# Two gate rows by way of DRAM and the rotary half-head swap by transfers within SBUF, in a four-layer block kernel

## What is computed

```python
x = x + gt1[:, None, :] * y
h = _modulate(_rmsnorm(x, norm_g[i, 1]), sh2, sc2)
x = x + gt2[:, None, :] * (jnp.square(jax.nn.relu(h @ mlp_w1[i])) @ mlp_w2[i])
```

```python
return jnp.concatenate([x1 * c - x2 * sn, x1 * sn + x2 * c], axis=-1).astype(x.dtype)
```

## Time and profile before

| | us |
|---|---|
| median of 3 runs | 1351.86 (1350.39 to 1352.41) |
| the profiled execution, its own time | 1350.53 |
| its span in the profile | 1348.8 |
| TensorE busy | 1303.3 |
| VectorE busy | 948.8 |
| ScalarE busy | 701.5 |
| GpSimd busy | 128.3 |

### The profile page before, as it was taken

The page is one execution under the profiler, slowest core; times in us unless marked ns, Lnnn a source line. Parts: engine busy times, 40 slices in busy tenths (PEclk is TensorE's granted clock), DMA queues, the critical chain, the costliest instruction groups (busy, mean ns, idle before and its releaser), DMA issues. The chain is left out here.

```text
span 1348.8 us, 24952 instructions
## 1 busy us (share of the span) xinstructions
PE 1303.3 (97%) x10507; PEld 1129.8 (84%) x10507; DVE 948.8 (70%) x1433; ACT 701.5 (52%) x1211; POOL 128.3 (10%) x133
## 2 busy tenths in 40 slices
PE   4999999999999999999999999999999999999997
PEld 2998888998899897788888887888888998888886
DVE  1887788976768776675566888666656677756655
ACT  2544544434567555564444648654445566644443
POOL 0000000010200764100000042000000021000000
PEclk9999999999999999999999999999999999999999
DMA  9996799995341012356665532465555543565561
GB/s 362 372 363 237 299 356 380 352 343 167 115 156 64 4 35 97 95 176 201 188 189 176 182 113 91 148 206 192 187 190 160 174 139 126 172 188 194 183 197 50
DMA packets 177575, 256.90 MB, mean 190 GB/s; under 512 B 10488, under 2 KB 122552, under 8 KB 177464
## 3 DMA queue, kind: packets, MB, share of 16 engines
q1 hardware_dynamic: 177464, 255.31, 56.8%
HBM read 254.25 MB, written 1.05 MB: 189 GB/s over the span
## 5 line engine op out<-in xcount | busy, mean ns | idle before, releaser
L1514 DVE TENSOR_TENSOR w_lo<-stage,w_hi 128x1024 fp32r<-128x1024 f32 (+1 forms) x372 | 447.6, 1239 | 160.4 <-ACT w_hi L889 160.0
L889 ACT ACTIVATE w_hi<-stage 128x1024 fp32r<-128x1024 f32 (+1 forms) x378 | 380.1, 1049 | 211.7 <-PE acc L2318 191.9
L2316 PE MATMUL acc<-w_hi,z_hi 128*128 128x512 f32 x640 | 252.6, 395 | 1.6 <-DVE z_lo L1963 1.6
L2318 PE MATMUL acc<-w_hi,z_lo 128*128 128x512 f32 x640 | 249.4, 390 | 0.0
L2317 PE MATMUL acc<-w_lo,z_hi 128*128 128x512 f32 x640 | 249.2, 389 | 0.0
L2259 PE MATMUL un<-h_both,w_hi 128*128 128x256 f32 x736 | 214.3, 291 | 1.8 <-POOL w_lo L860 1.1
L2260 PE MATMUL un<-h_both,w_hi 128*128 128x256 f32 x736 | 208.1, 283 | 0.0
L2261 PE MATMUL un<-h_both,w_lo 128*128 128x256 f32 x736 | 208.0, 283 | 0.0
L2259 PEld LDWEIGHTS un<-h_both,w_hi 128*128 128x128 f32 x736 | 140.8, 191 | 9.5 <-issue 5.4
L2316 PEld LDWEIGHTS acc<-w_hi,z_hi 128*128 128x128 f32 x640 | 120.1, 188 | 27.8 <-issue 4.0
L2260 PEld LDWEIGHTS un<-h_both,w_hi 128*128 128x128 f32 x736 | 141.0, 192 | 1.2 <-issue 0.7
(11 more groups left out here) (393 smaller groups left out, 1886.0 us busy)
## 6 DMA issues: line engine op xcount, KB each, us to landing
stage<-in_mlp_w SPq DMA_DIRECT2D x64, 1024.0 KB
ada_buf<-in_ada_w SPq DMA_DIRECT2D x48, 1024.0 KB, 11.4
stage<-in_w_up SPq DMA_DIRECT2D x32, 1024.0 KB
stage<-in_w_down SPq DMA_DIRECT2D x32, 1024.0 KB
stage<-in_conv_w_in SPq DMA_DIRECT2D x12, 1024.0 KB
stage<-in_rw_w_rkv SPq DMA_DIRECT2D x12, 1024.0 KB
stage<-in_w_in_a SPq DMA_DIRECT2D x8, 1024.0 KB
stage<-in_w_kv_b SPq DMA_DIRECT2D x8, 1024.0 KB
```

The source lines that it names most:

```text
L889: A_(w_hi[u % 2][:, half, 0:n], stage[u % NSTAGE][:, half, 0:n], ACT.Copy).then_inc(hi_made, 1)
L1514: V.tensor_tensor(w_lo[u % 2][:, half, 0:n], stage[u % NSTAGE][:, half, 0:n], w_hi[u % 2][:, half, 0:n].bitcast(F32), ALU.subtract).then_i ...
L2316: MM(y, z_hi[:, kt, q], wh[:, i, :], start=(first and kt == 0), stop=False, skip_group_check=True)
L2318: ins = MM(y, z_lo[:, kt, q], wh[:, i, :], start=False, stop=(last and kt == KT - 1), skip_group_check=True)
```

## The change

The two gate rows of the first layer are no longer made by `row_of_columns`. After unit 8 of the convolution (slot 8) and after slot 26 of the first MLP, TensorE turns the eight columns into an 8 x 128 tile in PSUM, ScalarE copies that to `gate_tiles`, SyncE writes it to DRAM (ahead of units 15 and 33) and reads it back spread over 128 partitions (ahead of units 18 and 44). VectorE waits for `gate_spread` instead of `row_out`.

The eight rotation products on TensorE (two passes each) go. Instead SyncE moves the halves of heads within SBUF, four transfers of 32 partitions for each r, from `rope_in` to the new `rope_turned`. The sign moves into the sine table. The waits that the rotations brought on TensorE go with them. Three semaphores of VectorE waiting for itself become the chained wait that it uses elsewhere, and the constant table has a part of zeros (`still`) where the rotation matrix was.

```diff
+        SWAPPED_AHEAD = (U_KI + 6, U_KI + 7, U_KI + 8, U_KI + 9, U_QA + 6, U_QA + 7, U_OA + 4, U_OA + 5)
...
+        GATE_SETS = (2, 5)
+        GATE_AT = (8, 26)
+        GATE_KEPT_AT, GATE_SPREAD_AT = (15, 33), (18, 44)
...
+            def keep_gate(r):
+
+                sp.wait_ge(sem("row_out"), r + 1)
+                sp.dma_start(gate_kept[r].rearrange("(t q) -> t q", q=P), gate_tiles[:, :]).then_inc(sem("gate_written"), 16)
+
+            def spread_gate(r):
+
+                sp.wait_ge(sem("gate_written"), 16 * (r + 1))
+                sp.dma_start(gate_rows[r][:], gate_kept[r].unsqueeze(0).to_broadcast([P, D])).then_inc(sem("gate_spread"), 16)
+
+            def swap_halves(r):
+
+                n = 1 if r == ROPE_KI else 2
+                sp.wait_ge(un_free, freed(V_A + ROPE_USE[r]))
+                for g in range(4):
+                    to, src = 32 * g, 32 * (g ^ 1)
+                    sp.dma_start(rope_turned[r % 2][to:to + 32, 0:n, :], rope_in[r % 2][src:src + 32, 0:n, :]).then_inc(sem(f"rope_landed{r % 2}"), 16)
...
+                if u in GATE_KEPT_AT:
+                    keep_gate(GATE_KEPT_AT.index(u))
+                if u in GATE_SPREAD_AT:
+                    spread_gate(GATE_SPREAD_AT.index(u))
+                if u in SWAPPED_AHEAD:
+                    swap_halves(SWAPPED_AHEAD.index(u))
                 load_unit(u)
...
-            def rope(r, n, dst, bank=misc):
-                dve.wait_ge(rot_done, r + 1)
-                link(V.tensor_tensor(dst, bank[:, 0:n, :], bc4(sin_root, n), ALU.mult))
+            def rope(r, n, dst):
+                dve.wait_ge(sem(f"rope_landed{r % 2}"), 64 * (r // 2 + 1))
+                link(V.tensor_tensor(dst, rope_turned[r % 2][:, 0:n, :], bc4(sin_root, n), ALU.mult))
                 dve.wait_ge(cos_done, r + 1)
                 V.tensor_tensor(dst, dst, rope_c[:, 0:n, :], ALU.add).then_inc(rope_done, 1)
...
+            def turn_gate(r):
+
+                i = ADA_ORDER.index(GATE_SETS[r])
+                c0 = 8 * (GATE_SETS[r] % 6)
+                pe.wait_ge(ada_added, i + 1)
+                nc.tensor.transpose(ada_turns(i)[0:KT, 0:P], mods[0][:, c0:c0 + KT], ident).then_inc(row_done, 1)
...
-                if j == 9:
-                    pe.wait_ge(ada_added, 3)
-                    row_of_columns(0, mods[0][:, 16:24], acc[0], acc[1])
...
-            def rot(r, n, v):
-                pe.wait_ge(un_free, freed(v))
-                if r:
-                    pe.wait_ge(rope_done, r)
-                MM(misc[:, 0:n, :], rot_w, rope_in[r % 2][:, 0:n, :], start=True, stop=True).then_inc(rot_done, 1)
```

More of the change, by code:

```diff
@@ L45 @@
            "c", "final_g", "g_attn_a_2", "g_kv_2", "g_attn_b_2", "g_mlp_2", "g_final_2")
-CONST_PARTS = ((("ident", P), ("mean", P), ("ones", P), ("rot", P)),
+CONST_PARTS = ((("ident", P), ("mean", P), ("ones", P), ("still", P)),
                (("head_ones", P), ("head_mean", P), ("level_t", 6 * CHUNK), ("masks", 2 * CHUNK), ("eye", CHUNK), ("resets", SEQ),
@@ L92, in constant_table @@
     put("cos", np.tile(np.cos(ang), (4, 1)))
-    put("sin", np.tile(np.sin(ang), (4, 1)))
+    put("sin", np.tile(np.sin(ang), (4, 1)) * np.where(i % HD < HD // 2, -1.0, 1.0)[:, None])
     tok = np.arange(QT)[None, :, None] * P + i[:, None, None]
@@ L98, in constant_table, with build @@
     return t
-def build(nc, A, out):
+def build(nc, A, out, gate_kept):
     with ExitStack() as ctx:
@@ L162, in build @@
         c_rep = new("c_rep", [P, KT, 32])
+        gate_tiles = new("gate_tiles", [KT, P])
         def c_(name):
@@ L167, in c_ @@
             return const[i][:, lo - CONST_AT[i]:hi - CONST_AT[i]]
-        ident, mean_w, ones_w, head_ones, head_mean, rot_w = (c_(n) for n in ("ident", "mean", "ones", "head_ones", "head_mean", "rot"))
+        ident, mean_w, ones_w, head_ones, head_mean = (c_(n) for n in ("ident", "mean", "ones", "head_ones", "head_mean"))
         level_t = c_("level_t").rearrange("p (j q) -> p j q", j=6)
@@ L275, in build @@
         rope_in = [at(f"rope_in{i}", [P, 2, SEQ], r_off[3] + 2048 * i) for i in range(2)]
+        rope_turned = [at(f"rope_turned{i}", [P, 2, SEQ], tmp_off + 4096 + 2048 * i) for i in range(2)]
         rope_c = at("rope_c", [P, 2, SEQ], r_off[3] + 4096)
@@ L1043, in row_copy, with gate_out @@
                 A_(gate_rows[r][:, HALF:D], flat(high), ACT.Copy).then_inc(row_out, 1)
+            def gate_out(slot):
+                if slot in GATE_AT:
+                    r = GATE_AT.index(slot)
+                    act.wait_ge(row_done, r + 1)
+                    if r:
+                        act.wait_ge(gate_written, 16 * r)
+                    A_(gate_tiles[:, :], ada_turns(ADA_ORDER.index(GATE_SETS[r]))[0:KT, 0:P], ACT.Copy).then_inc(row_out, 1)
             def z_split(zc, j):
@@ L1070, in mlp @@
                             split_half(uu + 2, 1)
[L1071 to L1072 removed]
                         if m == 0:
                             copy_set(COPIED_AT.get(S_MLP + 2 * UPD * g + j))
+                            gate_out(S_MLP + 2 * UPD * g + j)
                         if g == 0 and m >= 2:
@@ L1609, in residual @@
                     g = gated_f if n == N_FIN1 else gated
-                    dve.wait_ge(row_out, row + 1)
+                    if row < len(GATE_SETS):
+                        dve.wait_ge(gate_spread, 16 * (row + 1))
+                    else:
+                        dve.wait_ge(row_out, row + 1)
                     link(V.tensor_tensor(g[:, k % 2, :], y, gate_rows[row][:, HALF * h:HALF * (h + 1)], ALU.mult))
@@ L2158, in rope_query @@
             def rope_query(j):
-                rope(ROPE_Q + j, 2, q_fm[:, 2 * j:2 * j + 2, :], un[(V_A + 5 + j) % 2])
+                rope(ROPE_Q + j, 2, q_fm[:, 2 * j:2 * j + 2, :])
             rope_query(0)
             select(rounds - rounds // 2)
-            V.tensor_scalar(sel_bias[:], score[:], 0.5 * TAKEN, NEG, ALU.is_gt, ALU.mult).then_inc(sem("keys_chosen"), 1)
-            dve.wait_ge(sem("keys_chosen"), 1)
+            link(V.tensor_scalar(sel_bias[:], score[:], 0.5 * TAKEN, NEG, ALU.is_gt, ALU.mult))
             pair_logits(0, 0)
@@ L2451, in turn_set @@
                     pe.wait_ge(ada_added, i)
+                for r in range(len(GATE_SETS)):
+                    if i == ADA_ORDER.index(GATE_SETS[r]) + 2:
+                        pe.wait_ge(row_out, r + 1)
                 for b in range(2):
@@ L2463, in ada_piece @@
                     turn_set(TURNED_AT[slot])
+                if slot in GATE_AT:
+                    turn_gate(GATE_AT.index(slot))
             def mlp(m, n):
```

52 lines of the change are left out of this document (13 added, 39 removed).

## The result

The changed kernel takes 1371.94 us, median of 4 runs (1371.13 to 1372.32), beside 1351.12 (1350.14 to 1352.41) for the kernel before on the same chip: a ratio of 1.0154, interval 1.0142 to 1.0166, or +20.8 us. The forecast was +14.0 and 1364.5, with a range that ended at 1372: the measured time lies at the very end of it. The sign, the place and the order of the terms hold; every term of the rope stretch was too small. The profiled execution took 1372.08, its span 1370.3.

What follows compares the result with a forecast made beforehand. The prediction took VectorE's ropes 4 to 7, made late by their swaps, to bound the stretch from 798 to 829 us. Gates -2.2, ropes +14.0 and clock +2.2 gave +14.0 on 1350.53: 1364.5 us, range 1353 to 1372.

Steps and rivals of the forecast that it cites:

- What bounds the kernel: Between 798 and 829 us VectorE's finishing of ropes 4 to 7 sets the end, not TensorE, though TensorE is 97% busy.
- Gates, -2.2: Gate rows 0 and 1 through DRAM instead of sixteen TensorE matmuls each: -2.2 us, bounds 0 and -3.6.
- The two steps: Savings on TensorE for each gate row: 0.7 us for row 0, 1.6 us for row 1, rounded together to -2.2.
- Ropes 0 to 3, 0: Removing the first four rotations from TensorE gives nothing, since VectorE is the chain at 798; bound 3.4 us.
- L: Time from issue of the load ahead of a swap to landing of its last transfer: 5.6 us, bounds 3.7 and 7.1.
- Ropes 4 to 6: Delays from late swaps, each from L and fixed distances: rope 4 +5.0 us, rope 5 +2.2, rope 6 +3.8.
- Rope 7, +3.0: Rope 7 starts later because its swap stands behind the load of U_KI+13: +3.0 us, range 1.1 to 4.5.
- The clock, +2.2: TensorE runs at half clock after the last pause ahead of ropes 4 to 7: +2.2 us, 0 to 4.4.
- the rival with 0.09: Clock falls after each of four pauses, and three other 2.2 us reach the chain: 1371 us; chance 0.09.
- Edits at nothing: Chained wait, VectorE's sine product reading SBUF instead of PSUM, and SyncE's sixteen more issues cost nothing.
- Short landing: Rival: query swaps don't queue behind the load, L 3.7, ropes +6.4: 1354.7 to 1357 us; chance 0.17.
- The faster rival: Swaps are hidden, so the kernel is faster: 1346.8 us, about 1342 if all eight rotations come back; chance 0.11.

Runs made afterwards that it cites:

- experiment 2's first kernel: Kernel before with the gate change, and only the query ropes 4 to 7 by transfers, at the changed kernel's places: 1370.6 us, 1.0143.
- experiment 7: Kernel before with the gate change, and each of the eight rotations on TensorE done twice: 1353.47 us, 1.0015.
- experiment 8: Two kernels with the gate change: only ropes 5 and 6 by earlier transfers, 1349.23 us; only rope 3 by transfers, gate row 0 sent back a unit earlier, 1348.01 us.
- experiment 6: Changed kernel with 16 spare matmuls on TensorE in the four pauses ahead of ropes 4 to 7: 1369.55 us, 1.0134.
- experiment 3: Changed kernel with swaps 4 to 7 each issued one unit load earlier in SyncE's order: 1357.69 us, 1.005.
- experiment 5: Changed kernel with the four transfers of each swap issued by ScalarE right behind its own copy: 1365.25 us, 1.0104.
- experiment 4: Changed kernel with swaps 4 to 7 issued after the same split wait, but the load behind the swap instead of ahead: 1364.39 us, 1.0099.
- row 0 earlier: Kernel before with the gate change for both rows, row 0 sent back ahead of unit 17 instead of 18, rotations as before: 1348.28 us, 0.998.
- experiment 1: Kernel before with the gate change alone, all rotations left on TensorE: 1349.02 us, 0.9987.
- row 1 alone: Kernel before with the gate change for row 1 only; row 0 and the rotations as before: 1350.01 us, 0.9993.
- second kernel of experiment 2: Kernel before with the gate change, and only ropes 1 to 3 by transfers, at the changed kernel's places: 1351.7 us, 1.0006.
- ropes 5 and 6 alone: Kernel before with the gate change, and only ropes 5 and 6 by transfers, issued one load earlier than in the changed kernel: 1349.23 us, 0.9987.

## Why the prediction was right, and where it wasn't

- **Where the time went.** In the profiled execution rope 0 starts 0.7 us sooner than before, the way from rope 0 to rope 3 is 1.35 longer, that from rope 3 to rope 7 19.3 longer, and that behind rope 7 1.5 longer: 21.45 of the 21.5. The forecast had -2.2, 0, 14.0 and 2.2.
- **What bounds the kernel.** Right from rope 4 on: the loss of experiment 2's first kernel is all there. Wrong before: "What the first four give I take as nothing, since VectorE is the chain at 798" read a chain that begins at 798 and carried it back to 770. By experiment 7 a rotation added there is time added; by experiment 8 one taken away gives half of its time back.
- **Gates, -2.2.** Measured -1.8 (-2.8 to -0.5), row 0's wait 0.87 for 0.9. At 337 us, behind both rows, TensorE is 2.2 us ahead of the kernel before (337.13 against 339.37 for the same matmuls); a dip of the clock right there takes 1.6 back ahead of rope 0 (the last section has its price in other profiles). The two steps, 0.75 and 1.65, sum to 2.4, which the prediction put down as 2.2. Not foreseen: the spread in SyncE's queue holds up a modulation piece by some 0.8 us.
- **Ropes 0 to 3, 0.** Measured +2.6 for ropes 1 to 3. VectorE idled 2.3 us ahead of rope 1, but 1.55 of idling stood there before: rope 1 starts 3.6 us after rope 0 instead of 2.6, so it is 0.9 us late (0 by my L, 1.2 by its upper bound; L was 6.8). Then the index scores waited for rope 2, and the clock fell. What the rotations gave, at most 2.6 us, was given back and as much again.
- **L, 5.6.** This is the term that was mis-sized. It measured 6.6 (798.83 to 805.40), 7.3 and 6.9, around the upper bound of 7.1. Both of its parts were too low. The traffic of load and swap, put at 4.45 + 0.7, ended 5.5 us after the load's issue for swap 4 (at about 804.3), 6.1 for swap 5 and 5.9 for swap 6. The part behind it, of which I let most lie under the load ("I take 0.5"), was 1.1, 1.2 and 1.0. The issues were too cheap as well (0.4 us each after the unit loads; a piece of a swap takes 0.5 to 0.6, four took 2.41), but they stand in the lower bound only, and end before the traffic does.
- **Ropes 4 to 6.** Each step is L plus a fixed distance, and with L as measured the chain follows: rope 4 should be 6.57 - 0.60, 6.0 late, and was done 6.65 late, of which 0.7 was rope 3's; rope 5's 5.73 + 7.35 - 9.17 gives 3.9 and was 3.8; rope 6's 5.94 + 6.94 - 7.72 gives 5.2 and was 5.0. The method was right, to 0.2 us.
- **Rope 7, +3.0.** Measured 4.5, by another way: its input was late, and the term became an input wait plus 3.8. That the clock had made the input late hardly mattered. In experiments 2 (the query ropes) and 6, where the input came 1.1 and 1.0 us sooner after rope 6, L was 6.7 and 6.8, which gives 4.99 + 6.75 - 7.60, 4.1: the late input is worth some 0.4, the rest is L.
- **The clock, +2.2 after the last pause only.** Nearly right. The dip after the last pause cost what lies between 20.0 and 21.5, 1.5 us, and 1.3 to 2.5 over five profiles. The dips ahead of it reached the chain through rope 7's input, the way that the rival with 0.09 named, but with some 0.4 us, not with 2.2 each: the cover by VectorE and GpSimd held. The Trainium skill (TensorE: Matmul & The Clock Gate, section on why it matters for kernels) has the rule that a pause puts the clock back: here the trace agrees with 0.50 behind all four, though not with a price for each.
- **Edits at nothing.** One wasn't. A sine product that reads SBUF twice took 1.53 beside GpSimd in experiments 3 and 8, and 0.84 for rope 0 against 0.41 before. By the Trainium skill (SBUF — State Buffer, section on its two separate sides) a VectorE instruction with two SBUF inputs and a GpSimd one that reads SBUF lock each other out for a whole instruction. The profiles fit that: in experiment 8 GpSimd's product runs from 813.95 to 815.22 and VectorE's, begun at 814.23, ends at 815.76; in experiment 5 VectorE's was first for rope 1 (776.29 to 776.97), and there GpSimd's, begun at 776.51, took 1.62 instead of 1.27. No run tests it by itself.
- **The rivals.** The number nearest to the result, 1371, belongs to the rival in which every pause has its price, but it isn't borne out: it had L at 5.6 and three more prices of 2.2, and the runs show L at 6.6 to 7.3 and some 0.4 for the three. Short landing was the wrong value of L, not a wrong idea: experiment 4 has it as soon as nothing stands in front. The faster rival, about 1342, was out of reach: with the places corrected, ropes 4 and 7 still wait, because 3.9 us is more than their inputs allow.

So the mechanism was right and its size was not: the forecast of +14.0 is two thirds of +20.8, and the time lies within the range by 0.1 us, because the range took in L's upper bound of 7.1, which by the prediction's sum gives 20.0 for the ropes where 19.3 was measured. That it lies within by so little is luck.

Open: how the 14 us split if each load were also kept on time, how much the clock took in all, and what rope 0's swap does alone. Swaps issued by GpSimd weren't tried.

## What to carry to other kernels

A small transfer that the next step needs costs its issues plus its landing plus whatever large load stands ahead in its queue: for four pieces 3.9 us alone and 6.6 to 7.3 behind one megabyte (8.7 once). So ask of each when its data are ready and when they are wanted; here, with under 4 us between the two, 0.86 us of an engine that stands by was cheaper, even though that engine is busy for 97%. And read the bound of a stretch in that stretch: here the engine on the chain changed within 30 us.

## What the runs showed of the hardware

The DMA view of the changed kernel (transfer, count, KB each, median us from issue to landing):

```profile
gate_row<-gate_kept SPq DMA_DIRECT2D x2, 512.0 KB, 9.5
...
rope_turned<-rope_in SPq DMA_DIRECT2D x28, 64.0 KB, 4.6
```

A row of 4 KB spread over 128 partitions landed after 8.1 and 10.9 us, where the 512 KB row took 5.5. And TensorE's clock can fall or not at the same place: around 336 us it pauses for about 1 us twice in both kernels, and the granted clock there was 1.00 in the kernel before and 0.75 and 0.50 in the changed one:

```profile
336.00:338.00 2.00, 1.00 (x5) 0.83 (x4) 1.90 (x6) 0.42 (x1) 0.07 (x1) 0.75 0.91 309
338.00:340.00 2.00, 2.00 (x6) 1.36 (x5) 1.93 (x5) 0.69 (x2) 1.19 (x2) 0.50 1.04 327
```

It doesn't follow the change: with the gates alone it stayed at 1.00, with row 0 earlier it fell to 0.50. Of the fourteen profiles, five have a dip there, four (experiments 1, 3, 6 and row 1 alone) have none there but one behind a pause of 1.5 us at 460, and five have neither. Each dip has a price. In the nine profiles with one, what TensorE was ahead of the kernel before at 337 us has shrunk by 1.3 to 1.7 us when rope 0 starts. In the second kernel of experiment 2, in experiment 7 and with ropes 5 and 6 alone, which have no dip up to there, it is the same within 0.1. (The other two without a dip are the kernel before itself and experiment 5, where rope 0 is late for another reason.)

Single executions of one kernel differ along with the clock too. Of the 15 executions of the kernel before beside experiment 1, the eight with a mean granted clock of 0.999 took 1349.8 to 1350.6 us, and the six with 0.996 or 0.997 took 1351.8 to 1353.0. So an effect under 1 us stays inside the intervals here, and a profile has to be read for where its clock fell before it is set beside another.
